# Down-projection of a decoder step: 32 of its 44 input tiles by the seven-product step

## The reference

```python
h = x + jnp.concatenate([att, y], axis=-1) @ w_out
f = rmsnorm(h, norm_ffn)
h = h + (jax.nn.silu(f @ w_gate) * (f @ w_up)) @ w_down
...
y_prompt = rmsnorm(hp, norm_final)
```

## Time and profile before

| what | us |
|---|---|
| runs of the kernel | 3020.83 median of 3 (3015.36 to 3022.0) |
| the profiled execution, its own time | 3024.53 |
| its span in the trace | 3022.4 |
| making of the activation operands, PE mostly idle | from 1402 to 1457 |
| gate and up products in the chain | 971.68 |
| down products in the chain, three pieces | 537.85, 12.80 and 12.78 |

### The profile page before, as it was taken

The page is one execution under the profiler, slowest core; times in us unless marked ns, Lnnn a source line. Parts: engine busy times, 40 slices in busy tenths (PEclk is TensorE's granted clock), DMA queues, the critical chain, the costliest instruction groups (busy, mean ns, idle before and its releaser), DMA issues.

```text
span 3022.4 us, 49649 instructions
## 1 busy us (share of the span) xinstructions
PE 2830.1 (94%) x20713; PEld 2694.1 (89%) x20713; DVE 1508.8 (50%) x2311; ACT 949.1 (31%) x1440; POOL 548.8 (18%) x230
## 2 busy tenths in 40 slices
PE   6999999999999986997899999999999999999997
PEld 5887898877777764996899999999999999999997
DVE  3312399544444445015766776766766633232223
ACT  4222221232333323223334344343333422222222
POOL 2222232211111100431000000000000033333331
PEclk9999999999999987998899999999999999999999
DMA  6422222555555545442232333333333352323221
GB/s 203 115 72 73 72 77 78 147 150 159 158 148 150 152 119 189 131 131 80 78 110 96 128 100 98 121 100 115 105 100 119 116 200 100 115 100 116 100 100 63
DMA packets 367372, 354.00 MB, mean 117 GB/s; under 512 B 40957, under 2 KB 321125, under 8 KB 365880
## 3 DMA queue, kind: packets, MB, share of 16 engines
q1 hardware_dynamic: 334136, 325.20, 34.0%
q10 hardware_dynamic: 33024, 25.77, 2.6%
HBM read 303.18 MB, written 49.13 MB: 117 GB/s over the span
## 4 chain that ended last, share of the span: by engine, by line
PE 57%; issue 31%; POOL 7%; DVE 2%; ACTq 1%; ACT 1%; POOLq 0%; DVEq 0%
PE PS L1230 32%; PE PS L1212 19%; PE PS L789 6%; POOL WL L692 4%; POOL WL L721 3%; ACTq L1274 0%; DVE XR L2264 0%; ACTq L1275 0%; DVE xo_t L2269 0%; DVE xo_x L2269 0%; DVE y_out L2339 0%; POOL WL L713 0%; ACT WRAW L1283 0%; DVE rstd L2257 0%; PE PS L804 0%
## 5 line engine op out<-in xcount | busy, mean ns | idle before, releaser
L789 PE MATMUL PS<-AH,WH 128*128 128x288 f32 (+1 forms) x2208 | 497.6, 308 | 30.1 <-DVE AL L2164 11.0
L1212 PE MATMUL PS<-H,WH 128*128 128x288 f32 x2816 | 489.5, 296 | 0.7 <-DVE us L2231 0.7
L789 PE MATMUL PS<-AL,WH 128*128 128x288 f32 (+1 forms) x2208 | 483.8, 302 | 0.0
L789 PE MATMUL PS<-AH,WL 128*128 128x288 f32 (+1 forms) x2208 | 482.3, 301 | 0.0
L711 POOL TENSOR_TENSOR WL<-WRAW,WH 128x1024 fp32r<-128x1024 f32 x88 | 213.9, 2431 | 1379.6 <-ACT WH L704 1379.6
L789 PEld LDWEIGHTS PS<-AH,WH 128*128 128x128 f32 (+1 forms) x2208 | 366.8, 195 | 56.4 <-issue 35.1
L1212 PEld LDWEIGHTS PS<-H,WH 128*128 128x128 f32 x2816 | 414.6, 189 | 0.9 <-issue 0.9
L1230 PE MATMUL PS<-xo_t,WH 128*128 128x288 f32 x1888 | 380.9, 296 | 7.8 <-ACT kept L1627 7.6
L789 PEld LDWEIGHTS PS<-AL,WH 128*128 128x128 f32 (+1 forms) x2208 | 367.0, 194 | 0.0
L789 PEld LDWEIGHTS PS<-AH,WL 128*128 128x128 f32 (+1 forms) x2208 | 365.5, 194 | 0.0
L2325 DVE TENSOR_TENSOR XD<-PS,XD 128x576 f32<-128x576 f32 x176 | 133.4, 758 | 398.8 <-PE PS L1212 398.8
(11 more groups left out here) (351 smaller groups left out, 3786.2 us busy)
## 6 DMA issues: line engine op xcount, KB each, us to landing
WRAW<-in_w_gate SPq DMA_DIRECT2D x22, 2048.0 KB
WRAW<-in_w_up SPq DMA_DIRECT2D x22, 2048.0 KB
WRAW<-in_w_down SPq DMA_DIRECT2D x22, 2048.0 KB
WRAW<-in_w_in SPq DMA_DIRECT2D x14, 2048.0 KB, 8.4
raw<-in_w_in SPq DMA_DIRECT2D x48, 512.0 KB, 4.1
kca<-in_cache_k SPq DMA_DIRECT2D x256, 64.0 KB, 2.8
vca<-in_cache_v SPq DMA_DIRECT2D x256, 64.0 KB, 2.0
WRAW<-in_w_out SPq DMA_DIRECT2D x16, 1024.0 KB
```

Source lines behind the costliest of these rows:

```text
L789: last = nc.tensor.matmul(G[gslot][0:width, h, 0:HALF], wt[:, half, k % 8, 0:width], act[:, (k + shift) % KT, h * HALF:(h + 1) * HALF], st ...
L1212: last = mm(G[(slot + t) % 2][:, h, 0:HALF], wt[:, half, 2 * k + t, :], hid[:, m, k, h * HALF:(h + 1) * HALF], start=(k == 0 and wt is WH ...
```

## The change

The first 32 input tiles of the down-projection are taken as two chunks of 16 tiles (2048 rows of `w_down`). Each chunk is done in eight passes of the same seven-product step, 256 output columns each: passes 44 to 51 and 52 to 59, so there are 60 passes (`NALL`) and 420 products. The remaining 12 tiles are three groups of the old form (`NL`).

Each chunk needs its own seven activation operands. They are made while PE works, around the first pass of the chunk: SP loads quarter blocks of the hidden tiles from `hS` into free halves of the operand tiles, and `turn_high` (ACT) and `turn_low` (DVE) make them between the preparations of products. n counts products from the chunk's first one. The first two passes of a chunk are interleaved in the order `TURNED`, so that operands are wanted later. PE waits for each operand through `x_lo`.

The output sums of a pass start from DRAM: SP loads two tiles of `xrS` into `gs2` or `us2`, `gather` adds the kept state and the PSUM bank to them (two adds where one stood), and SP stores them back. The second chunk loads the sums again, and the last groups load them as `XD`.

```diff
+        FIRST = (NPAIR, NPAIR + 8)
+        TURNED = ((0, 0), (0, 1), (0, 3), (0, 2), (0, 5), (1, 0), (1, 1), (0, 4), (1, 3), (1, 2), (0, 6), (1, 5), (1, 4), (1, 6))
...
+            for e, q in enumerate(FIRST):
+                c = 7 * q
+                load_weights(q)
...
+                hidden_part(e, "C", 0, 1, 2)
+                if e:
+                    store_sums(q - 2)
+                    next_sums(q - 2)
+                sp.wait_ge(s["p_done"], c - 6)
+                hidden_part(e, "x00", 0, 0, 0)
+                sp.wait_ge(s["p_done"], c - 5)
+                hidden_part(e, "x10", 1, 0, 1)
+                sp.wait_ge(s["p_done"], c - 4)
+                hidden_part(e, "D", 1, 1, 3)
+                load_weights(q + 1)
+                sp.wait_ge(s["p_done"], c)
+                hidden_part(e, "t4", 1, 0, 4)
...
+                for r in range(q + 2, q + 8):
+                    load_weights(r)
+                    store_sums(r - 2)
+                    next_sums(r - 2)
...
+            def turn_low(e, n):
+
+                def go(name, k, src=None):
+                    dve.wait_ge(s["x_hi"], 7 * e + 7 + k)
+                    tt(xo[name][:, 1, :, :], x_raw[src or name][:, :, :], xo[name][:, 0, :, :].bitcast(F32), ALU.subtract).then_inc(s["x_lo"], 1)
+
+                def sub(dst, a, b, k):
+                    tt(x_raw[dst][:, :, :], x_raw[a][:, :, :], b, ALU.subtract).then_inc(s["x_p"], 1)
+                    dve.wait_ge(s["x_p"], 5 * e + k)
+                if n == -3:
+                    dve.wait_ge(s["p_done"], 7 * FIRST[e] - 3)
+                    dve.wait_ge(x_in[2], 16 * e + 32)
+                    dve.wait_ge(x_in[0], 16 * e + 32)
+                    sub("t1", "C", x_raw["x00"][:, :, :], 1)
+                if n == -2:
+                    go("x00", 1)
+                if n == -1:
+                    go("x10", 2)
+                if n == 0:
+                    dve.wait_ge(x_in[3], 16 * e + 32)
+                    sub("t2", "D", x_raw["t1"][:, :, :], 2)
+                    go("t1", 3)
+                    sub("t3", "D", x_raw["C"][:, :, :], 3)
+                    go("x11", 4, "D")
+                if n == 1:
+                    go("t2", 5)
+                if n == 4:
+                    go("t3", 6)
+                if n == 6:
+                    dve.wait_ge(x_in[4], 16 * e + 32)
+                    sub("t4", "t4", xo["t2"][:, 0, :, :].bitcast(F32), 4)
+                    sub("t4", "t4", xo["t2"][:, 1, :, :].bitcast(F32), 5)
+                if n == 8:
+                    go("t4", 7)
```

More of the change, by code:

```diff
@@ L365, in build @@
         NPAIR = HID // P
-        NPROD = 7 * NPAIR
+        NALL = NPAIR + 16
+        NPROD = 7 * NALL
         LOOP0 = 12
-        TL, CL = TF + 16 * (NG - 1), CD + 8 * (NG - 1)
+        G0, NL = 8, NG - 8
+        TL, CL = TF + 16 * (NL - 1), CD + 8 * (NL - 1)
+        FIRST = (NPAIR, NPAIR + 8)
+        TURNED = ((0, 0), (0, 1), (0, 3), (0, 2), (0, 5), (1, 0), (1, 1), (0, 4), (1, 3), (1, 2), (0, 6), (1, 5), (1, 4), (1, 6))
+        seq = []
+        for q in range(0, NALL, 2):
+            seq += [(q + d, j) for d, j in TURNED] if q in FIRST else [(q + d, j) for d in range(2) for j in range(7)]
+        POS = {v: c for c, v in enumerate(seq)}
+        ADD = {v: n + 1 for n, v in enumerate(v for v in seq if v[1] in (1, 4, 5, 6))}
+        KEEP = {v: n + 1 for n, v in enumerate(v for v in seq if v[1] in (0, 2, 3))}
+        RAW = {}
+        for q, j in seq:
+            for what in {0: ("difference",), 2: ("second", "fourth"), 3: ("sum",)}.get(j, ()):
+                RAW[q, what] = len(RAW) + 1
+        assert all(POS[q, 6] == max(POS[q, j] for j in range(7)) for q in range(NALL))
         D_AT = {1: 0, 2: 1}
@@ L1265, in back @@
                     made(last, name)
-            group_pe(NG - 1, 0, lambda h: back((h - 3) // 2) if h in (3, 5, 7) else None)
+            group_pe(NL - 1, 0, lambda h: back((h - 3) // 2) if h in (3, 5, 7) else None)
             back(3)
@@ L1617, in cast @@
                 if j >= 2 and j < 6:
-                    act.wait_ge(s["p_raw"], 4 * q + (2, 4, 1, 3)[j - 2])
+                    act.wait_ge(s["p_raw"], RAW[q, ("second", "sum", "difference", "fourth")[j - 2]])
                 copy(w_high(r), operand(up, j, r)).then_inc(s["p_hi"], 1)
@@ L2226, in gather @@
                 src = F[up][:, BANK[j], 0:HALF]
-                dve.wait_ge(s["p_done"], 7 * q + (j + 1))
-                if up and j == 1 and not (isinstance(q, int) and q == 1):
+                dve.wait_ge(s["p_done"], POS[q, j] + 1)
+                kept_in = None if n is None else KEEP[q, (0, 2, 3)[n]]
+                if q >= NPAIR:
+                    if j == 1:
+                        dve.wait_ge(xt_in[up], 8 * (q - NPAIR - up) + 144)
+                    if n is not None:
+                        parts_added[0] += 1
+                        dve.wait_ge(s["e_cp"], kept_in)
+                        tt(dst, dst, kept[:, n, :], ALU.add).then_inc(s["e_part"], 1)
+                        dve.wait_ge(s["e_part"], parts_added[0])
+                    tt(dst, dst, src, ALU.add).then_inc(s["e_add"], 1)
+                    return
+                if up and j == 1 and q > 1:
                     dve.wait_ge(s["h_st"], 8 * (q - 1))
@@ L2304, in low_hidden @@
+            for c in range(5, NPROD):
+                q1, j1 = seq[c - 1]
+                if c + 2 < NPROD:
+                    q2, j2 = seq[c + 2]
+                    prepare(c + 2, q2, j2, (c + 2) % 3, q2 % 2, lambda: gather(q1, j1, q1 % 2))
+                else:
+                    gather(q1, j1, q1 % 2)
+                for e, q in enumerate(FIRST):
+                    turn_low(e, c - 7 * q)
             def low_hidden(g, b, j):
```

215 lines of the change are left out of this document (132 added, 83 removed).

## The result

The changed kernel takes 3024.53 us (median of 20 runs, 3019.11 to 3035.43), the kernel before 3017.83 us on the same chip (20 runs, 3013.83 to 3025.04). The ratio is 1.0024 with a 95% interval of 1.0014 to 1.0033, so it is slower by 6.7 us. The forecast was 3024.6 us, "no change that can be told"; the truth lies at the border of that class, on its slow side.

The account below looks back on a forecast made before the run. PE was taken to bound both stages. Terms of -52.7 + 27.3 + 27.8 + 0.5 + 0.9 = +3.8 us on 3020.83 gave 3024.6 us, with an 8-in-10 range of 3009 to 3041 us.

Parts of the forecast that it names:

- PE's saving and the steady passes: Chunk passes: fewer matmuls save PE 52.7 us; the 12 passes away from the chunks' beginnings add nothing.
- The beginnings: Each chunk's first products: VectorE's twelve large instructions make PE wait, 27.3 us in the first chunk, 27.8 in the second.
- The busy share over the whole stage: All 16 passes: VectorE at 89%, under its limit; by that rule the whole -52.7 us would arrive.
- rival 1: Chunks: VectorE keeps up, 2969.5 us, chance 0.04; a likelier part of it, 3003 to 3013 us, chance 0.16.
- Start of the down groups: Before the down groups' first product: four low parts (3 us) ahead of the last gather add about 0.5 us.
- the prediction's section on the clock: Chunk beginnings: PE's longer stops halve the clock, costing 2.6 us each on the fourth and tenth products.
- The load of `hraw1`: First down group: the load waits behind the last store of sums, +0.9 us, bounds 0 and 3.
- Sum: Whole kernel: all terms together give +3.8 us, 3024.6 us for the median, no change that can be told.
- rival 3: First two products of each chunk: short waits also lower the clock, +9.0 us, 3029.8 us; chance 0.17.
- rival 4: Chunk beginnings: a block of hidden tiles lands late, each 5 us later, +13.8 us, 3034.6 us; chance 0.10.
- The clock rival: Chunk beginnings: the clock stays up, so they cost 23.7 and 24.1 us; 3017 us, chance 0.10.

Follow-up runs that it names:

- no_vector: Changed kernel with VectorE's twelve large instructions per chunk cut to 128 x 8 elements; 2973.13 us, ratio 0.9856 to the kernel before.
- best: Changed kernel with VectorE's list and stores reordered, one t4 difference, dummy transposes, first hidden group's parts earlier; 3000.20 us, ratio 0.9944 to the kernel before.
- the second comparison: The unmodified changed kernel measured again beside the kernel before; 3021.28 against 3018.53 us, ratio 1.0008.

## Why the prediction came out as it did

- **PE's saving and the steady passes: right.** 22.31 us a pass still (the same VectorE row of two successive passes at 2535.72 and 2558.03 us), no gap of PE in twelve of sixteen passes, second adds hidden.
- **The beginnings: right in mechanism, places and size.** 26.4 and 27.0 us against 27.3 and 27.8. The stops were forecast at 0.9, 0.85, 5.9, 6.1, 4.4 and 1.3 us and measured at 0.87, 0.47, 5.71, 6.24, 4.33 and 1.31; in the second chunk they were 1.23, 1.00, 5.11, 6.58, 4.32 and 1.32, the first two forecast at 1.5 and 1.4. The fourth and the tenth product lost 1.8 and 2.7 us to the clock, where 2.6 each were forecast. That it is VectorE's list was a reading of queues; no_vector showed it.
- **The busy share over the whole stage misled.** It came out as costed: VectorE was busy for 316.25 us against the 357 us of the products, 89%. Read as the prediction did (the Trainium skill, page Perfetto Trace Analysis, section Identifying the Most-Contended Engine, takes this share as a fair measure of how close VectorE is to its limit), the whole -52.7 us should have arrived. The trace agrees with it only where it is taken over a beginning alone: there VectorE leads, with 67.12 of 78 us against PE's 59.07. It takes no_vector to get 2973.1 us; rival 1 had this at 2969.5.
- **Start of the down groups: the term was mis-sized.** The step "about 0.5 us more" than 0.67 became 3.47 us, and 1.5 us of slow clock behind it, which the prediction's section on the clock doesn't have, so 4.3 us for 0.5. It took four low parts at 3 us, by their time when alone. GpSimd's subtractions held them. The trace of before had shown it in two multiplies of 0.75 us beside GpSimd, which I had read over:

```profile
2429.12 3.63 DVE L2239 TENSOR_TENSOR us<-us,gs 128x576 f32<-128x576 f32 x2
2429.75 2.39 POOL L711 TENSOR_TENSOR WL<-WRAW,WH 128x1024 fp32r<-128x1024 f32 x1 [0.74 <-ACT WH L704]
```

- **The load of `hraw1`: expected +0.9 us, was 0.** The mechanism was right and the room for it larger than thought. It was issued at 2844.95, 8.2 us behind the start of the down groups instead of just ahead of it, but landed 6.6 us later where it had taken 14.5. ScalarE waited 5.52 us, GpSimd was done with the low part of the fourth half at 2855.6, and PE came to it at 2857.7, 1.5 us later than at the full clock. In best, where PE starts sooner and its first tile is not slow, the term is there: the stop of 0.9 us on GpSimd's low part.
- **Sum.** In the same terms: -52.7 + 26.4 + 27.0 + 2.8 = +3.5 us, with the slow first tile +5.0, and the traces' bookkeeping gives +4.8. The median moved by 6.7, with an interval of 4 to 10 us, and by 2.8 in the second comparison. The sum was right to a few us; the class was decided by less than the terms were uncertain. That the forecast time (3024.6 us) meets the median (3024.53) to 0.1 us is luck: it was added to 3020.83 us for the kernel before, whose 20 runs here give 3017.83, and the measured difference is larger by as much.
- **The rivals.** Short stops did not bring the clock down (rival 3): a first product in 3.50 us at 2423.15. No block was late (rival 4): the only waits for x blocks were ScalarE's, 1.4 us in two. The clock rival was right in size (24.0 and 24.2 us when it stays up) and wrong only in whether it does.

## What to carry to other kernels

When a change adds large instructions to an engine that has time on average, lay its queue out by products or tiles around the place where they stand, beside what the next engine wants: a burst of 30 us in a window of 38 costs PE what does not fit, whatever the busy share. If a removed piece of that queue gives nothing, look for the bound right behind it (here a weight slot that came free late, seen through one gather), and remove both. Before work goes to an idle engine, look in the trace for instructions of the two that overlap in time, and compare their lengths with the ones that don't.

## What the hardware showed that was not expected

- In the overlaps shown here, VectorE and GpSimd subtractions with both operands in SBUF did not run at once. VectorE's 1.22 us became 6.15 behind GpSimd's 5.26, four of 0.75 us became 7.18 across two of GpSimd's, and GpSimd's 5.26 became 7.08 when VectorE's was first.
- The granted clock fell to 0.50 within a stop of 5.7 us and was back at 1.00 before the product behind it was done. Dummy transposes in the stops kept it up and were worth 5.2 us for two beginnings; where other work of the same length lay beside the slow products, 1.5 us.
- The unchanged first 1450 us of the program took from 1446.9 to 1459.1 us in the traces of these kernels, more than most effects looked for here. The stretch between two events, traced twice for one kernel, differed by 0.6 us.
